# Scores of two query blocks in one group in three branches of a decoder trunk, and what is moved with them

## What is computed

```python
def hybrid_layer(x, ...):
    h = split_cols(x @ w_in)
    out_a = causal_dense_attention(qa, ka, va, ..., decay)            # A, forgetting attention
    out_b = mla_attention(h['b_cq'], h['b_ckv'], h['b_kr'], ...)      # B, latent; rotary part of 32
    out_c = dsa_sparse_attention(q, k, v, iq, ik, iw, ..., top_k)     # C, top 256 keys of a query
    out_d = sliding_window_sink_attention(q, k, v, ..., sinks)        # D, window of 128, 2 blocks of keys
    mixed = concatenate([out_a * silu(a_g), out_b * silu(b_g), out_c * silu(c_g), out_d * silu(d_g)])
    return layer_norm(ALPHA * x + mixed @ w_out, ln_g, ln_b)
```

## Time and profile before

| | |
|---|---|
| median of 3 runs | 2945.43 us (2944.47 to 2949.46) |
| the profiled execution | 2943.56 us |
| its span | 2941.6 us |
| PE busy | 2854.4 us, 97% of the span |
| DVE, ACT, Pool busy | 1621.2, 1059.6, 642.6 us |
| layer 0: branches A, D, B, C | about 239 to 529, 529 to 776, 776 to 1025, 1025 to 1284 us |
| layer 1: D, C | about 1998 to 2240, 2484 to 2720 us |

### The profile page before, as it was taken

How to read it: one execution, slowest core, us unless ns; L and a number is a source line. 1 busy time by engine, 2 the same in 40 slices (tenths; PEclk the granted TensorE clock), 3 DMA queues, 4 the chain that set the end, 5 groups by cost and what they waited for, 6 DMA issues and landing times. The chain is left out here.

```text
span 2941.6 us, 39580 instructions
## 1 busy us (share of the span) xinstructions
PE 2854.4 (97%) x13638; PEld 1675.1 (57%) x13638; DVE 1621.2 (55%) x4361; ACT 1059.6 (36%) x3085; POOL 642.6 (22%) x1336
## 2 busy tenths in 40 slices
PE   7999999999999999999999999999999999999998
PEld 5446666555566666644544466665555666665443
DVE  5337888767776433322333388886767764323232
ACT  3334444343455345500012334443334544445000
POOL 1002333111122244500000022331112222444000
PEclk9999999999999999999999999999999999999999
DMA  6201111111110121042120011111011101201421
GB/s 225 66 8 47 44 44 33 38 33 45 37 32 19 33 99 33 26 149 79 58 91 31 10 45 44 44 33 45 28 43 37 33 17 33 106 28 30 155 86 43
DMA packets 90908, 156.88 MB, mean 53 GB/s; under 512 B 11296, under 2 KB 67248, under 8 KB 88920
## 3 DMA queue, kind: packets, MB, share of 16 engines
q1 hardware_dynamic: 90712, 154.36, 16.4%
HBM read 120.13 MB, written 32.08 MB: 52 GB/s over the span
## 5 line engine op out<-in xcount | busy, mean ns | idle before, releaser
L1160 PE MATMUL ps_s<-xT,w_ring 128*128 128x348 f32 (+4 forms) x3616 | 1122.4, 464 | 12.6 <-DVE gate L1617 5.0
L1160 PEld LDWEIGHTS ps_s<-xT,w_ring 128*128 128x128 f32 x3616 | 673.3, 191 | 396.4 <-issue 102.6
L1412 ACT ACTIVATE arena<-ps_t 16x32 f32<-16x32 f32 (+3 forms) x1048 | 367.2, 373 | 239.9 <-PE ps_t L1230 225.7
L1399 ACT ACTIVATE arena<-arena,small 128x1040 f32<-128x1040 f32 (+8 forms) x544 | 372.0, 684 | 132.4 <-DVE small L1679 131.6
L1442 DVE MAX8 small<-score 128x8 f32<-128x1040 f32 (+6 forms) x448 | 376.3, 840 | 10.5
L1444 DVE MATCH_REPLACE8 score<-small,score 128x1040 f32<-128x1040 f32 (+6 forms) x448 | 370.0, 826 | 0.0
L1230 PE MATMUL ps_t<-ident,arena 128*128 128x128 f32 (+1 forms) x2016 | 300.5, 278 | 13.0 <-ACT arena L1412 12.9
L1791 POOL TENSOR_SCALAR strips<-arena,small 128x16 f32<-128x16 f32 x384 | 107.1, 279 | 902.2 <-DVE small L1691 902.2
L1203 PE MATMUL ps_s<-feat 64*128 64x272 f32 (+12 forms) x1680 | 295.6, 454 | 3.3 <-ACT arena L1315 3.2
L1230 PEld LDWEIGHTS ps_t<-ident,arena 128*128 128x128 f32 (+1 forms) x2016 | 224.2, 140 | 116.6 <-issue 67.0
L1794 POOL TENSOR_SCALAR arena<-arena,small 128x1024 f32<-128x1024 f32 (+7 forms) x384 | 286.2, 745 | 0.0
(11 more groups left out here) (177 smaller groups left out, 2504.8 us busy)
## 6 DMA issues: line engine op xcount, KB each, us to landing
w_ring<-in_w_feat SPq DMA_DIRECT2D x78, 512.0 KB, 3.5
mixed<-mixg SPq DMA_DIRECT2D x128, 128.0 KB, 1.7
feat<-mixed SPq DMA_DIRECT2D x16, 1024.0 KB, 6.7
resid<-score SPq DMA_DIRECT2D x16, 512.0 KB, 3.2
score<-resid SPq DMA_DIRECT2D x16, 512.0 KB, 7.6
arena<-in_w_out SPq DMA_DIRECT2D x4, 1536.0 KB, 8.0
cT<-falls SPq DMA_DIRECT2D x8, 520.0 KB, 4.8
feat<-falls SPq DMA_DIRECT2D x8, 520.0 KB, 5.2
```

What stands on the lines that cost most here:

```text
L1160: mm = pe.matmul(ps_s[:, bank, 0:w], w_ring[:, wt % 2, k, :], xT[:, k, c0:c0 + w], start=(k == 0), stop=(k == KT - 1))
L1399: nc.scalar.activation(p, p, ACT.Exp, scale=-1.0, bias=nm[:, e:e + 1], accum_out=psums[0:M, st % 4, e:e + 1]).then_inc(S["exp_done"], 1)
L1412: a = nc.scalar.activation(dst, src, ACT.Copy)
```

## The change

1. `rounds_of`: In D's pairs 0 to 2 the blocks are taken as [8, 7], [6, 5], [4, 3], [2, 1], [0]; in B and C singly to 4 and then [3, 2], [1, 0]. The scores of a round's blocks are made in one `qk` item, the maxima after them. The rest of a step (exponentials, transposes, fill work) still follows step by step. In D the reciprocals and norms of the round before stand ahead of a round's scores; at the other places they stand behind the scores, as before. `row_of` gives two blocks of a round one row.
2. B's blocks 3 and 2 have one product for each head in place of two.
3. `TOP_RATE` of D: 5 in the first three steps; a row of its own for D's last pair.
4. The latents: scaling and transposes of a token block come a step later (`LATENT_STEPS`), the 16-row block's projection two steps earlier; the rotation's third part comes a step later; B's later q_latents two steps later.
5. C's gate and next-query chunks are cut into halves of 4 products and spread over steps 0 to 8.
6. The opening norm: normalised in place, by ACT except for the first block (DVE), with −mean·rstd from two more ops on Pool; 20 more transposes of the identity on PE ahead of everything; DVE's memset moved behind the opening; one small ACT op ahead of the rest.

```diff
-TOP_RATE = {"A": [3, 4, 5, 5, 6, 4, 5, 5, 1], "D": [4, 4, 4, 4, 4, 4, 4, 4, 4],
+TOP_RATE = {"A": [3, 4, 5, 5, 6, 4, 5, 5, 1], "D": [5, 5, 5, 4, 4, 4, 4, 4, 4], "D3": [4, 4, 4, 4, 3, 2, 2, 2, 3],
...
+LATENT_STEPS = [[([0], []), ([1], [0]), ([2], [1])], [([3], [2]), ([4], [3]), ([5], [4])],
+                [([8, 6], [5]), ([7], [8]), ([], [6])]]
...
+def rounds_of(br, p):
+    if br == "D" and p < NP - 1:
+        return [[8, 7], [6, 5], [4, 3], [2, 1], [0]]
+    if br in "BC":
+        return [[8], [7], [6], [5], [4], [3, 2], [1, 0]]
+    return [[i] for i in ORDER]
...
-        products = even(n, 2 if n >= 272 else 1)
+        products = even(n, 2 if i > 3 else 1)
...
-                put(0, lambda: self.latent(l, NB - 2))
-                for idx in (1, 2):
-                    fill[idx].insert(0, lambda c=idx - 1: self.q_rope(l, 0, c, bank=self.free_bank()))
+                fill[1].insert(0, lambda: self.latent(l, NB - 2))
+                put(1, lambda: self.q_rope(l, 0, 0, bank=self.free_bank()))
+                fill[2].insert(0, lambda: self.q_rope(l, 0, 1, bank=self.free_bank()))
...
-                for idx, step in ((5, 0), (6, 1), (6, 2), (7, "dup")):
+                for idx, step in ((5, 0), (6, 1), (7, 2), (7, "dup")):
...
-                for idx, work in zip((3, 4, 5), self.q_latent(l, p + 1)):
+                for idx, work in zip((3, 4, 5) if p == 0 else (5, 6, 7), self.q_latent(l, p + 1)):
...
-            for idx, work in zip((3, 4, 5), self.tile(l, "Q", br="C", p=p + 1)):
+            rest = self.halves(l, "G", br=br, p=p) + self.halves(l, "Q", br="C", p=p + 1)
+            for idx, work in zip((0, 0, 1, 1, 2, 3, 4, 5, 6, 7, 7, 8), rest):
                 put(idx, work)
...
+        for blocks in rounds_of(br, p):
+            if l == DEPTH - 1 and 0 in blocks:
+                blocks = blocks[:-1]
+            steps = [self.step(l, br, p, i, hu) for i in blocks]
+            if len(steps) > 1 and br == "D":
+                self.normalise()
...
+            if steps:
+                self.add("qk", l=l, br=br, p=p, idx=steps[0]["idx"], hu=hu, steps=steps, ready=steps[0]["ready"])
+                self.normalise()
+                self.values()
...
+            self.rec_next += steps
...
+            for _ in range(20):
+                pe.transpose(ps_t[:, 0, 0:BLK], ident[:], ident[:])
...
+                elif kind == "ln" and 0 < it["ln"] < NB:
+                    ln, M, r = it["ln"], rows_of(it["b"]), it["ln"] % 2
+                    act.wait_ge(S["ln_rs"], ln + 1)
+                    nc.scalar.activation(x_in[ln][0:M, :], x_in[ln][0:M, :], ACT.Identity, scale=rstd[0:M, r, 0:1],
+                                         bias=rstd[0:M, r, 1:2]).then_inc(S["ln_act"], 1)
```

More of the change, by code:

```diff
@@ L290, in open, with chunk @@
         return self.take("wt")
-    def chunk(self, l, wt, what, c, bank=P_BANK, **kw):
+    def chunk(self, l, wt, what, c, bank=P_BANK, k1=KT, **kw):
         pieces = IQ_CHUNKS if what == "IQ" else (CHUNKS if what in ("IK", "AK", "K") else asked(l))
@@ L296, in chunk, with halves @@
         gin = self.take("gin") if what == "G" else (self.take("gin") if what == "IK" else None)
-        self.add("mt", l=l, what=what, wt=wt, cols=pieces[c], last=self.left[wt] == 0, gin=gin,
+        return self.add("mt", k0=0, k1=k1, l=l, what=what, wt=wt, cols=pieces[c], last=self.left[wt] == 0, gin=gin,
                  **self.group("dve" if what in ("G", "IK") else "act", bank, scored=what != "G"), **kw)
+    def halves(self, l, what, **kw):
+        out, wt = [], self.open()
+        for c in (2, 1, 0) if what == "G" else range(3):
+            begun = {}
+            out.append(lambda c=c, begun=begun: begun.update(self.chunk(l, wt, what, c, k1=KT // 2, **kw)))
+            out.append(lambda begun=begun: self.add(**dict(begun, k0=KT // 2, k1=KT)))
+        return out
     def tile(self, l, what, **kw):
@@ L541, in empty_step @@
         self.gated()
-        self.add("top", l=l, count=TOP_RATE[br][NB - 1])
+        self.add("top", l=l, count=top_rate(br, p)[NB - 1])
         between = 0 if br == "D" else 1
@@ L579, in normalise @@
     def normalise(self):
[L580 to L582 removed]
+        for s in self.rec_next:
+            self.add("rec", **s)
+        self.rec_next = []
     def flush(self, more=()):
@@ L785, in build @@
         for it in items:
-            if it["kind"] == "mt" and it["what"] == "G":
+            if it["kind"] == "mt" and it["what"] == "G" and it["k1"] == KT:
                 at = it["nth"]
@@ L1527, in _ @@
+                    if ln >= NB + 2:
+                        dve.wait_ge(x_st[r], 16 * len([n for n in range(ln - 1) if n % 2 == r]))
                         if it["xprev"]:
```

316 lines of the change are left out of this document (176 added, 140 removed).

## The result

| | before | changed |
|---|---|---|
| median | 2945.76 us (4 runs) | 2980.28 us (2977.45 to 2984.46, 4 runs) |
| ratio, 95% interval | | 1.0119 [1.0107, 1.0131] |
| profiled execution, its span | 2943.56, 2941.6 us | 2981.06, 2979.1 us |
| PE busy, rest of the span | 2854.4, 87.2 us | 2848.0, 131.1 us |

The account below looks back on a forecast made before the run. PE, busy 97% of the span, bounds the kernel, so only its work and waits count. Terms −4 − 4.8 − 17.9 + 28 + 5 − 6.6 − 8.4 = −8.7 us give a median of 2937 us, range 2916 to 2954.

Parts of the forecast that it names:

- Merging, −4.8 in D: D's score groups: two steps' scores in one group save 0.20 us, 24 times, −4.8 us.
- Rival 3: Score groups: the fixed 0.20 us is each product's own, merging saves nothing, 2947 us; chance 0.09.
- (a): D's last blocks: two blocks' norm behind Pool's second chain makes PE wait about 2.9 us a pair, +17.7 us.
- (b): D's round [6, 5]: blocks 8 and 7 normalised at its start make PE wait 1.2 to 1.4 us, +9.6 us.
- Rival 1: D: new waits half as long and nothing falls to the lower clock, 2918 us; chance 0.16.
- (c): D: lower clock after two of twelve new waits, 2.4 us each, +5 us.
- D, waits that go: D: waits for latent scaling and for ACT's copies at D's end go, with lower clock behind them, −17.9 us.
- Sum for D: D, both layers: merging, removed waits, new waits and clock together, about +10 us.
- Rival 2: D: each of 12 new waits is followed by 1.2 GHz, 2.4 us each, up to 2961 us; chance 0.17.
- B, −6.6: B: merged score groups save 3.6 us and 0.77 us waits for ACT go, 3.0 us, together −6.6 us.
- C, −8.4: C: merging −2.1, ACT waits −4.8, lower clock −3, last pair's halves +1.5, together −8.4 us.
- Start, −4: Opening norm: PE's waits at the first blocks shrink as ACT takes most normalising, −4 us (−1 to −7).

Follow-up runs that it names:

- what was found on the way: Kernel before plus opening norm, C's halved chunks, latent scaling ahead of top ops, and 28 top ops in D's last pair: 2917.71 us, ratio 0.9908.
- the opening alone: Kernel before with only the opening norm and C's halved chunks of the change: 2929.61 us, ratio 0.9943.
- repaired rounds and all ops: Kernel before plus opening norm, C's halves, D's rounds with first block's norm between steps, top rates 3/5, last pair's 36 ops kept: 2933.03 us.

## Why the prediction was wrong, by its own steps

- **Bound.** Right: the loss is PE's waits, 44 us of them, against 6 us less work.
- **Merging, −4.8 in D.** Right in size. The merged group runs 623.34 − 622.27 = 1.07 us up to the next; before there were two groups of 0.63. Rival 3 (no saving) fell. The Trainium skill's page "TensorEngine Tiling (Array Packing)" gives each matmul a cost of its own under "Instruction Overhead"; by that alone the merged group would take 1.26 us, and the trace has 1.07. In B it paid less than half of the 3.6: with rounds and no stretch at the lower clock (the run with the rotation as before) B, with the border's 1.8 us, is 3.0 and 4.2 us longer than one by one, while its waits are 3.9 and 4.4 us more. In C it did not pay.
- **(a) The last blocks' norm, +17.7.** Right: 2.95, 2.94, 3.33 and 3.09, 3.09, 3.48, in sum 18.9.
- **(b) Round [6, 5], +9.6.** 1.12 in each pair of layer 0, near the 1.2 worked out, and nothing more in the first pair; in layer 1 0.25 to 0.39, where gate waits of 2.0, 2.4 and 1.3 us had come ahead of it. 4.2 in sum, so this term was over twice too large. Rival 1 (all new waits half as long) fell on (a).
- **(c) Clock, +5.** The prediction took two of twelve new waits, 2.4 us each. Each of the six long ones of (a) was followed by the lower clock, with 1.7 us lost, 10.2 in all; the six of (b), 1.12 us and less, were not.
- **The missing term, and the first step that failed.** The sum asked for each new order only who normalises whom. It didn't ask what the removed scores had stood between. Two projection chunks follow each other on one bank, read by DVE or ACT in between; before, 0.63 us of scores on PE and one block's maxima on DVE stood there. 13.3 us of gate waits and 4.9 more of squares waits came of it, and no rival had them. The prediction's last paragraph names waits "behind DVE's pairs of maxima" as a sign of being wrong, but gives them no price. Who is queued behind the moved instruction was asked for Pool and not for DVE: the second block's maxima move ahead of the top ops and so ahead of the gate.
- **D, waits that go, −17.9.** The second step that failed. The 3.38 went, but the scaling of the last full block, moved one step, stood behind four top ops of a step in which PE had little to do: 4.04 where 1.56 had been. D's end turned 3.05 into 0.82 + 2.60, by the copy that the prediction had named, so nothing was won there. In all, of 16.1 us of such waits in both layers 15.0 stayed. Nor did the lower clock go: (1 − granted clock) × time rose from 3.4 to 6.8 us in D of layer 0 and from 6.8 to 8.5 in layer 1. One of its places:

```profile
580.00:590.00 10.00, 7.05 (x32) 3.84 (x31) 5.95 (x19) 3.79 (x16) 3.15 (x8) 0.83 0.23 70
```

- **Sum for D.** PE is idle 20.4 and 21.2 us more, and busy 0.8 more in layer 0 and 1.2 less in layer 1: 41.2, as measured. The busy part is the merging, 2.4 less each, against at most 3.4 and 1.7 more of lower clock. The forecast was about 10.
- **Rival 2 (the lower clock behind each wait).** It had the sign and a small part of the cause: six of its twelve waits were followed by the lower clock, but other places had it before, so that it took 5.1 us more in D, of the 41.
- **B, −6.6, measured +7.1 (+8.9 with the border).** The waits of 0.77 us for ACT went, but others of 0.40 came, so that ACT's are 4.6 us where they were 4.8. And waits of 0.4 to 0.9 for Pool came, two or three in most pairs, since two blocks' norms are put side by side: waits 5.8 to 14.1 us in both layers, the DMA's at B's start not counted.
- **C, −8.4, measured −5 (−7 with the border).** The halves gave what was expected of the waits (8.8 without rounds, and there the 0.77 goes without blocks 1 and 0 scored together); the term of merging had the wrong sign, about +4.5 in place of −2.1.
- **Start, −4, measured −5.9.** Right, in the range given; the same opening gave −3.2 to −6.5 in the other kernels.

## What to carry to other kernels

When work is taken from between two uses of one buffer, it was cover for whoever empties the buffer; price the gap, not only the work. Moving work of one engine forward moves everything of that item on all engines: write the queue of each of them before and after, also where the diff says nothing. And a wait that is removed is worth what stands behind it: a norm wait here hid a gate wait, and the copies' wait a DMA's. Undo the parts one by one, since a slow change may hold a fast one (here 0.6% from two parts, 0.9% with what was found on the way).

## What the chip showed beside

The lower clock does not follow from a wait's length alone. At D's end of layer 0 the kernel before waits 3.05 us and does the 12 products after it in 1.09 us; the versions with the opening alone, and with repaired rounds and all ops, wait the same at the same place (3.04 and 3.05), and the 12 products last 1.98 in both. In the first of them:

```profile
767.04 1.98 PE L1308 MATMUL ps_o<-arena 128*64 128x256 f32 x12 [3.04 <-ACT arena L1484]
```

So a single profile's time at the lower clock can differ by some 3 us at one place for a reason that isn't in the edit, and by 11 us over the program, as B's and C's blocks one by one show (33.9 against 22.6). Waits, in contrast, repeat to a few hundredths from kernel to kernel, and are the better thing to compare.
